# One-hots of the first index moved to ScalarE in every batch, the build and the dense stage re-placed in the row order

## The chip, the core and the metric

The kernel runs on one core of a Trainium2 chip. The core has TensorE (PE), VectorE (DVE), ScalarE (ACT), GpSimd (POOL) and SyncE (SP), which run side by side and meet at semaphores, and 16 DMA engines that all queues share. The metric is the device time of one execution in microseconds (us); lower is better.

## What is computed

A one-layer streaming encoder in float32 for 512 prompt tokens and 64 sample tokens, width 2048: retention and mLSTM heads, then the PEER expert mixer, then gated per-layer embeddings. The change touches the expert mixer. For every token, 8 heads pick 16 of 16384 experts each (128 picks); the expert number is `i1 * 128 + i2`. Cut to what matters:

```
eidx = i1 * N_KEYS + i2            # (T, 128) expert numbers, N_KEYS = 128
act  = gelu(einsum('td,tkd->tk', xb, u[idx]))      # one row of peer_u for each pick
out  = einsum('tk,tkd->td', g * act, v[idx])       # one row of peer_v for each pick
```

## The kernel before

Tokens lie in 5 blocks of 128 (block 4 is the sample block, its 64 tokens laid out twice, so it has 64 picks per partition). A "row" is one pick of all 128 tokens of a block: GpSimd gathers 128 vectors of 2048 floats from `peer_u` (1 MiB) into a slot of `ring`. VectorE takes the dot product with the token (L2330), and for blocks 0, 3 and 4 it later adds the gathered row of `peer_v` to the token's sum (L2342, 12 rows behind). Rows are numbered 0 to 575; block 2 is rows 256 to 383, block 3 rows 384 to 511, block 4 rows 512 to 575. From row 384 on the `peer_u` rows use three slots of the ring and the `peer_v` rows three others.

Blocks 1 and 2 (`DENSE`) do without the second gather. Their weights are made dense: for each token a matrix of 128 x 128 (first index by second index) that holds the weight of each picked expert. This is the **build**. It goes in batches of four tokens, 32 batches (`PER`) for each of the two blocks, `b` 0 to 63. A batch is:

- VectorE compares the indices with `iota` and makes one-hots (L2204). In even batches it makes those of both indices (128 x 1024), in odd ones only those of the second (128 x 512).
- ScalarE makes the first index's one-hots in odd batches as `relu(1 - |index - iota|)`: four Abs (L1644) and one Relu (L1647). It then scales the second one-hots by the weights, four instructions (L1657).
- TensorE multiplies the two (L1206), ScalarE copies the product of the batch before out of psum (L1679).
- Every four batches 1 MiB goes to `a_scratch` in HBM, half issued by SP and half by ACT (L764).

Three sets of one-hot buffers go round (`SETS`), so the compare of batch `b` waits for the multiplication of batch `b - 2` (L2201), and so do ScalarE's Abs.

The **dense stage** then reads all of `peer_v` once, in 32 groups `m` of four 1 MiB tiles. For each group TensorE multiplies tiles by weights (L1223) in four parts, VectorE adds each part (L2221), and SP loads the group after next only when a group is done. Weights come back in 16 chunks (L783). TensorE is at most three parts ahead of VectorE. After the dense stage comes the gated embedding product of blocks 0 to 3 (`pe_embed`, L1265) in four groups, whose sigmoids are ScalarE's (L1725) and whose sums are VectorE's (L2240, L2244).

Each engine runs one stream of instructions in order, written by weaving several generators (`braid`). A step yields a place in row numbers, and the step with the lowest place is written next. `BUILD_AT` gives for each dense block the first row and the rows per batch, `DENSE_AT` the first row of the dense stage and the rows per group, `EMBED_AT`, `EMBED_RS` and `GROUP_ROWS` the places of the embedding's steps. So these numbers set only the order on VectorE and ScalarE; how long it takes is decided by waits.

Of the kernel before, what the change touches and what calls it, by code (L numbers as in the profile page):

```python
# [14 lines left out]
P = 128  # L15
# [45 lines left out]
BATCH = 4  # L61
# [8 lines left out]
ALONE = (128, 384)  # L70

CHAIN_AT = {0: (-89, 4.0), 1: (12, 4.7), 2: (138, 8.7)}
EMBED_AT = {0: (533, 1.05), 1: (700, 1.0)}
FIRST_PICK = {1: 4.0, 2: 10.0}
LATE_PICKS = {1: [(131, 10), (148, 16), (170, 18), (200, 18), (222, 18), (246, 18), (270, 18)],
              2: [(402, 9), (424, 18), (450, 20), (472, 9), (481, 9), (490, 9), (499, 9)]}
BUILD_AT = ((352, 0.9), (390, 0.55))
DENSE_AT = (412, 3.75)
GROUP_ROWS = (548.5, 10.5)
EMBED_RS = 541.5  # L80

def in_at(g, x):
# [44 lines left out]
def build_at(d, x):  # L128
    return BUILD_AT[d][0] + BUILD_AT[d][1] * x

def dense_at(x):
    return DENSE_AT[0] + DENSE_AT[1] * x

def embed_at(e, x):
    return EMBED_AT[e][0] + EMBED_AT[e][1] * x

# [221 lines left out]
def build(nc, a, out):  # L360
    with ExitStack() as ctx:
# [41 lines left out]
        def bank(n, width=512):  # L403
            return psum[:, n, 0:width]

        far, ident, keep, fold = (misc[:, x:x + P] for x in (M_FAR, M_ID, M_KEEP, M_FOLD))
        iota, iota_p, one = misc[:, M_IOTA:M_IOTA + NC], misc[:, M_IOTA:M_IOTA + P], misc[:, M_ONE:M_ONE + 1]
# [148 lines left out]
        def one_hots(b):  # L556

            at = 1024 + b % SETS * 1024
            return (X if b >= PER else Wf)[:, at:at + 1024].rearrange("p (f t i) -> p f t i", f=2, t=BATCH)
# [9 lines left out]
        def stored(i, w):  # L569

            return 32 * len(range(i, w, SETS))
# [80 lines left out]
        f0 = y0 = len(EMBEDS[0])  # L652
# [984 lines left out]
        def act_build(act):  # L1637
            def first_hots(d, b):

                if b >= SETS:  # L1640
                    act.wait_ge(a_mm, b - SETS + 1)
                for x in range(BATCH):
                    t = b % PER * BATCH + x
                    ins = act.activation(one_hots(b)[:, 0, x, :], iota_p, ACT.Abs, bias=build_parts(d)["indexT"][:, t:t + 1], scale=-1.0)  # L1644
                act_o.did(ins)
                act_o.wait()
                act_o.did(act.activation(one_hots(b)[:, 0], one_hots(b)[:, 0], ACT.Relu, bias=1.0, scale=-1.0))  # L1647

            def weigh(d, b):

                if b % 2:
                    first_hots(d, b)
                act.wait_ge(hots, b + 1)
                for x in range(BATCH):
                    t = b % PER * BATCH + x
                    hot = one_hots(b)[:, 1, x, :]
                    ins = act.activation(hot, hot, ACT.Identity, scale=build_parts(d)["weightT"][:, t:t + 1])  # L1657
                ins.then_inc(weighed, 1)
            for d in range(len(DENSE)):
                yield build_at(d, -1)  # L1660
                act.wait_ge(index_t, d + 1)
                act.copy(build_parts(d)["indexT"], bank(6)[:, 0:2 * P])
                act.copy(build_parts(d)["weightT"], bank(7)[:, 0:P]).then_inc(index_c, 1)
                for i in range(PER + 1):
                    b = d * PER + i
                    if i < PER:
                        yield build_at(d, i + 0.1)
                        if i == 0:
                            act.wait_ge(index_c, d + 1)
                        weigh(d, b)  # L1670
                    if i == 0:
                        continue
                    b -= 1
                    yield build_at(d, i + 0.2)
                    act.wait_ge(a_mm, b + 1)
                    w, t0 = b // WRITE, b % WRITE * BATCH
                    if w >= SETS and t0 == 0:
                        act.wait_ge(a_out[w % SETS], stored(w % SETS, w))
                    act.copy(a_stage(w)[:, :, t0:t0 + BATCH, :].rearrange("p c t k -> p t c k"),  # L1679
                             bank(b % 4).rearrange("p (t c k) -> p t c k", t=BATCH, k=CHUNK)).then_inc(a_c, 1)  # L1680
                    if b % WRITE == WRITE - 1:
                        act.wait_ge(a_c, b + 1)
                        store_a(act, w, 1)
# [14 lines left out]
        def act_embed(act):  # L1698
# [4 lines left out]
            for q in range(4):  # L1703
                for j, t in enumerate(ts):
# [7 lines left out]
                    act.activation(spare, hrow(t), ACT.Square, accum_out=ncol(i, 0)).then_inc(n_sq, 1)  # L1712
            yield EMBED_RS
            act.wait_ge(n_ms, rooted(counts.stat["ple", 0, 0]))
# [463 lines left out]
        def dve_build(dve):  # L2178
            o = dve_o
            for d, t in enumerate(DENSE):  # L2180
                parts = build_parts(d)
                yield build_at(d, -2)
                if d:
                    dve.wait_ge(moved, 2)
                    dve.wait_ge(picked[3], 1)
                else:
                    dve.wait_ge(mm, prod.end("q", 2))
                dve.wait_ge(weighted, (ROW0[t] + ROWS[t]) // GRP)
                o.wait()
                o.did(dve.tensor_scalar(parts["first_u"].bitcast(U32), eidx[:, eslot(t), :], 7, None, ALU.logical_shift_right))  # L2190
                o.did(dve.tensor_scalar(parts["second_u"].bitcast(U32), eidx[:, eslot(t), :], NKEY - 1, None, ALU.bitwise_and))
                o.wait()
                o.did(dve.tensor_copy(parts["first_f"], parts["first_u"].bitcast(U32)))
                dve.tensor_copy(parts["second_f"], parts["second_u"].bitcast(U32)).then_inc(split, 1)
                for i in range(PER):
                    b = d * PER + i
                    yield build_at(d, i)
                    if i == 0:
                        dve.wait_ge(index_c, d + 1)
                    if b >= SETS:  # L2200
                        dve.wait_ge(a_mm, b - SETS + 1)  # L2201
                    index = parts["indexT"].rearrange("p (f t o) -> p f t o", f=2, o=1)[:, :, i * BATCH:(i + 1) * BATCH, :]
                    f0 = b % 2
                    dve.tensor_tensor(one_hots(b)[:, f0:, :, :], index[:, f0:, :, :].to_broadcast([P, 2 - f0, BATCH, P]),  # L2204
                                      iota_p.rearrange("p (a b i) -> p a b i", a=1, b=1).to_broadcast([P, 2 - f0, BATCH, P]),
                                      ALU.is_equal).then_inc(hots, 1)

        def dve_dense(dve):
# [14 lines left out]
        def dve_embed(dve):  # L2223
            ts, n = EMBEDS[0], len(EMBEDS[0])

            def at(x):
                return embed_at(0, x)
            yield EMBED_RS
            dve.wait_ge(n_sq, counts.stat["ple", 0, n - 1] + 1)
            dve.tensor_scalar(embed_cols(1), embed_cols(0), 1.0 / D, EPS, ALU.mult, ALU.add).then_inc(n_ms, 1)  # L2230
            yield EMBED_RS + 0.6
            dve.wait_ge(n_rt, rooted(counts.stat["ple", 0, 0]))
# [147 lines left out]
```

## Time and profile before

| | us |
|---|---|
| median of 3 runs | 3673.85 (3673.23 to 3678.76) |
| the profiled execution, its own time | 3674.24 |
| span of its instructions | 3672.4 |
| PE busy | 3098.5 |
| VectorE busy | 2748.2 |
| GpSimd busy | 1301.3 |
| ScalarE busy | 642.8 |

The span is the time from the first to the last instruction; 1.8 us lie around it. Busy times overlap, since the engines run side by side. All times below are counted from the start of the span. The DMA engines moved 1453.00 MB in all.

### The profile page before, as it was taken

To read this page: it belongs to the slowest core of one execution; us is meant where nothing else is said; L and a number is where in the kernel's file an instruction comes from. 1 tells how busy PE (TensorE), PEld (TensorE's weight loads), DVE (VectorE), ACT (ScalarE), POOL (GpSimd) and SP (SyncE) were. 2 spreads that over 40 slices of the span, in tenths; PEclk is the share of its full clock that TensorE was granted. 3 is DMA by queue.
4 is the path that set the end of the run, shared out by engine and by line. 5 is a ranking of instruction groups with operands and counts; after the bars stand their busy time and mean duration, and the time that the engine had idled before them with its cause. 6 is when DMAs were issued, how large, how long until landed. Compare 5 with 4: busy or idle time off the path is not lost.

```text
span 3672.4 us, 26507 instructions
## 1 busy us (share of the span) xinstructions
PE 3098.5 (84%) x9234; PEld 1897.2 (52%) x9234; DVE 2748.2 (75%) x3646; ACT 642.8 (18%) x1694; POOL 1301.3 (35%) x908
## 2 busy tenths in 40 slices
PE   8998697999988189899897545699999999799697
PEld 4447443554456144455347544466666666574343
DVE  1014987767668799888778888878788999777885
ACT  2211210222011031122202367200000000003002
POOL 0001542424335443323234533432323323342771
PEclk9999799999989589999898755699999999899899
DMA  8889999999999999999999999999999999999998
GB/s 272 282 274 326 418 417 417 419 417 419 418 413 407 381 390 417 417 418 384 378 416 404 400 383 388 389 421 422 421 421 422 419 421 418 389 421 415 417 401 354
DMA packets 310517, 1453.00 MB, mean 396 GB/s; under 512 B 26032, under 2 KB 64368, under 8 KB 172272
## 3 DMA queue, kind: packets, MB, share of 16 engines
q0 software_dynamic: 129840, 944.83, 62.9%
q1 hardware_dynamic: 153728, 485.39, 34.4%
q10 hardware_dynamic: 26816, 21.09, 1.7%
q8 instruction: 73, 1.20, 0.1%
q14 instruction: 60, 0.49, 0.0%
HBM read 1424.48 MB, written 26.74 MB: 395 GB/s over the span
## 4 chain that ended last, share of the span: by engine, by line
DMA 44%; DVE 18%; PE 14%; issue 6%; POOL 4%; ACT 1%; DVEq 0%; SPq 0%; ACTq 0%
DMA ring<-in_peer_u,eidx 23%; DMA ring<-in_peer_v,eidx 15%; DVE ring L2330 8%; DMA W<-in_w_peer_q 5%; PE psum L911 5%; DVE arena L2342 4%; POOL ring L843 4%; PE psum L1265 3%; PE psum L1223 3%; PE psum L1174 1%; DVE arena L2221 1%; DMA a_scratch<-W 1%; PE psum L1312 1%; DMA W<-in_w_out 1%; DVE arena L2204 1%
## 5 line engine op out<-in xcount | busy, mean ns | idle before, releaser
L2330 DVE CUSTOM_DVE_ANT_0 ring<-ring,cx 128x2048 f32<-128x2048 f32 x576 | 1315.2, 2287 | 301.5 <-DMA ring<-in_peer_u,eidx 298.6
L843 POOL DMA_INDIRECT ring<-in_peer_u,eidx x576 | 825.3, 1433 | 1609.9 <-DVE dots L2330 1194.1
L2342 DVE SCALAR_TENSOR_TENSOR arena<-ring,wts,arena 128x2048 f32<-128x2048 f32 x320 | 752.3, 2351 | 185.0 <-DMA ring<-in_peer_v,eidx 156.8
L911 PE MATMUL psum<-W,actT 128*128 128x512 f32 x1792 | 799.7, 605 | 45.3 <-ACT actT L858 21.0
L843 POOL DMA_INDIRECT ring<-in_peer_v,eidx x320 | 470.8, 1471 | 671.9 <-DVE arena L2342 633.4
L911 PEld LDWEIGHTS psum<-W,actT 128*128 128x128 f32 x1792 | 344.6, 194 | 467.6 <-issue 449.9
L1174 PE MATMUL psum<-actT,W 128*128 128x128 f32 (+2 forms) x1536 | 293.4, 356 | 97.8 <-DMA W<-in_w_peer_q 89.0
L1174 PEld LDWEIGHTS psum<-actT,W 128*128 128x128 f32 x1536 | 267.4, 211 | 123.3 <-DMA W<-in_w_peer_q 97.1
L1796 ACT ACTIVATE gel<-dots 128x8 f32<-128x8 f32 x72 | 15.2, 212 | 1610.1 <-DVE dots L2330 1605.6
L1223 PE MATMUL psum<-arena 128*128 128x512 f32 x512 | 233.0, 614 | 36.2 <-DVE arena L2221 36.2
L911 PE MATMUL psum<-W,arena 128*128 128x512 f32 x512 | 230.9, 612 | 21.1 <-DMA W<-in_w_out 20.6
L1223 PE MATMUL psum<-W,actT 128*128 128x512 f32 x512 | 225.8, 601 | 21.2 <-DMA actT<-a_scratch 16.9
L1223 PE MATMUL psum<-arena,actT 128*128 128x512 f32 x512 | 226.2, 600 | 12.0 <-DVE arena L2221 12.0
L1223 PE MATMUL psum<-W,arena 128*128 128x512 f32 x512 | 225.0, 599 | 8.6 <-DVE arena L2221 8.6
L1223 PEld LDWEIGHTS psum<-arena 128*128 128x128 f32 x512 | 159.9, 315 | 108.3 <-DVE arena L2221 41.4
L1223 PEld LDWEIGHTS psum<-W,actT 128*128 128x128 f32 x512 | 159.9, 314 | 85.9 <-issue 25.6
L1223 PEld LDWEIGHTS psum<-arena,actT 128*128 128x128 f32 x512 | 159.8, 314 | 76.8 <-DVE arena L2221 17.3
L889 PE MATMUL psum<-W,actT 128*128 128x512 f32 x448 | 198.8, 602 | 0.0
L1223 PEld LDWEIGHTS psum<-W,arena 128*128 128x128 f32 x512 | 159.9, 314 | 72.7 <-issue 10.5
L911 PEld LDWEIGHTS psum<-W,arena 128*128 128x128 f32 x512 | 99.7, 197 | 148.3 <-issue 120.8
L2221 DVE TENSOR_TENSOR arena<-psum,arena 128x1024 f32<-128x1024 f32 x128 | 155.9, 1218 | 18.0 <-PE psum L1223 17.9
L1265 PE MATMUL psum<-W,actT 128*128 128x512 f32 x256 | 118.3, 614 | 32.5 <-ACT arena L1725 32.5
(332 smaller groups left out, 2526.8 us busy)
## 6 DMA issues: line engine op xcount, KB each, us to landing
W<-in_w_in SPq DMA_DIRECT2D x168, 1024.0 KB, 12.3
W<-in_peer_v SPq DMA_DIRECT2D x64, 1024.0 KB
arena<-in_peer_v SPq DMA_DIRECT2D x64, 1024.0 KB, 16.8
W<-in_w_out SPq DMA_DIRECT2D x48, 1024.0 KB, 16.7
W<-in_w_peer_q SPq DMA_DIRECT2D x48, 1024.0 KB, 27.7
W<-in_w_ple_gate SPq DMA_DIRECT2D x24, 1024.0 KB, 16.0
ring<-in_peer_u,eidx POOLq DMA_INDIRECT x576, 18.2
actT<-a_scratch SPq DMA_DIRECT2D x8, 1024.0 KB, 28.0
```

What stands on the lines that cost most here:

```text
L843: pool.indirect_dma_start(ring[:, slot, :], None, a["peer_u" if what == "u" else "peer_v"][0], off(ix, 0)).then_inc(ring_in[slot], 16)
L889: ins = pe.matmul(bank(4 * s + j), lhs(k, j), W[:, k, :], start=(k == 0), stop=(k == KT - 1))
L911: ins = pe.matmul(bank(4 * s + j), lhs(at_k, j), w_pair(q)[:, k, s * CG:(s + 1) * CG], start=(at_k == 0), stop=(at_k == KT - 1))
L1174: ins = pe.matmul(bank(2 * (i % 2) + c // 2)[:, at:at + fresh], W[:, k, c * P:(c + 1) * P], actT[:, k, 0:fresh], start=(k == 0 and c % 2 = ...
L1223: ins = pe.matmul(bank(at % 3 * 2 + half), a_chunk(c)[:, i // 2 * P:(i // 2 + 1) * P, m * VT % CHUNK + x], v_tiles(m)[:, x, c0:c0 + 512], ...
L1265: ins = pe.matmul(bank(j), aT(k, j), W[:, k, :], start=(k == 0), stop=(k == KT - 1))
L1312: ins = pe.matmul(psum[SAMPLE * b:SAMPLE * (b + 1), s, :], actT[:, k, 0:SAMPLE], w_row(k)[:, cols_of(s, b)], start=(k == 0), stop=(k == KT ...
L1796: act.activation(gel[:, n % DEEP, :], dots[:, n % DEEP, :], ACT.Gelu).then_inc(gelud, 1)
L2204: dve.tensor_tensor(one_hots(b)[:, f0:, :, :], index[:, f0:, :, :].to_broadcast([P, 2 - f0, BATCH, P]), iota_p.rearrange("p (a b i) -> p a ...
L2221: dve.tensor_tensor(hc, psum[:, at % 3 * 2:at % 3 * 2 + 2, :], hc, ALU.add).then_inc(d_add, 1)
L2330: dve.tensor_tensor_reduce(row, row, cx[:, :], 1.0, 0.0, ALU.mult, ALU.add, dots[:, n % DEEP, c:c + 1]).then_inc(u_used, 1)
L2342: dve.scalar_tensor_tensor(out=hslot(t), in0=ring[:, slot, :], scalar=wts[:, n % DEEP, c:c + 1], in1=hslot(t), op0=ALU.mult, op1=ALU.add). ...
```

## The change

Four numbers of the order change, and the one-hots of the first index are ScalarE's in all batches.

```
-EMBED_AT = {0: (533, 1.05), 1: (700, 1.0)}
+EMBED_AT = {0: (536, 1.05), 1: (700, 1.0)}
...
-BUILD_AT = ((352, 0.9), (390, 0.55))
-DENSE_AT = (412, 3.75)
+BUILD_AT = ((352, 1.15), (396, 0.7))
+DENSE_AT = (423, 3.5)
...
-EMBED_RS = 541.5
+EMBED_RS = 543.5
...
             def weigh(d, b):
 
-                if b % 2:
-                    first_hots(d, b)
+                first_hots(d, b)
                 act.wait_ge(hots, b + 1)
...
-                    f0 = b % 2
-                    dve.tensor_tensor(one_hots(b)[:, f0:, :, :], index[:, f0:, :, :].to_broadcast([P, 2 - f0, BATCH, P]),
-                                      iota_p.rearrange("p (a b i) -> p a b i", a=1, b=1).to_broadcast([P, 2 - f0, BATCH, P]),
+                    dve.tensor_tensor(one_hots(b)[:, 1:, :, :], index[:, 1:, :, :].to_broadcast([P, 1, BATCH, P]),
+                                      iota_p.rearrange("p (a b i) -> p a b i", a=1, b=1).to_broadcast([P, 1, BATCH, P]),
                                       ALU.is_equal).then_inc(hots, 1)
```

In the changed file lines after the ScalarE edit are one lower, those after the VectorE edit two lower.

VectorE's stream at the first batches of block 1 (row 352). `W` holds the one-hots; an ISA row with `ring,dots` is one `peer_u` row. Before:

```order
L2204 TENSOR_TENSOR W<-W,misc 128x1024
L2204 TENSOR_TENSOR W<-W,misc 128x512
L2330 ISA ring,dots<-ring,cx 128x2048
L2330 ISA dots 128x1
L2204 TENSOR_TENSOR W<-W,misc 128x1024
```

In the changed kernel:

```order
L2202 TENSOR_TENSOR W<-W,misc 128x512
L2328 ISA ring,dots<-ring,cx 128x2048
L2328 ISA dots 128x1
L2202 TENSOR_TENSOR W<-W,misc 128x512
L2328 ISA ring,dots<-ring,cx 128x2048
```

Every compare is now of the short form, and with 1.15 rows per batch two seldom stand together; the last four batches of block 1 move behind the start of block 3 at row 384.

VectorE's stream at the first batches of block 2 (`arena` holds the one-hots there). Before:

```order
L2204 TENSOR_TENSOR arena<-arena,misc 128x1024
L2204 TENSOR_TENSOR arena<-arena,misc 128x512
L2330 ISA ring,dots<-ring,cx 128x2048
L2330 ISA dots 128x1
L2204 TENSOR_TENSOR arena<-arena,misc 128x1024
L2204 TENSOR_TENSOR arena<-arena,misc 128x512
```

In the changed kernel:

```order
L2202 TENSOR_TENSOR arena<-arena,misc 128x512
L2334 TENSOR_TENSOR wts<-gel,gate 128x8
L2340 SCALAR_TENSOR_TENSOR arena<-ring,wts,arena 128x2048
L2202 TENSOR_TENSOR arena<-arena,misc 128x512
L2328 ISA ring,dots<-ring,cx 128x2048
L2328 ISA dots 128x1
L2202 TENSOR_TENSOR arena<-arena,misc 128x512
```

Two compares stood between two `peer_u` rows (rows 390 to 396 have no `peer_v` rows yet); now the compares begin at row 396, among rows of both kinds.

ScalarE's stream at the first batches of block 1. Before:

```order
L1657 ACTIVATE W<-W 128x128 x4
L1644 ACTIVATE W<-misc,W 128x128 x4
L1647 ACTIVATE W<-W 128x512
L1657 ACTIVATE W<-W 128x128 x4
L1679 COPY W<-psum 128x4x16x8
L1657 ACTIVATE W<-W 128x128 x4
L1679 COPY W<-psum 128x4x16x8
```

In the changed kernel:

```order
L1644 ACTIVATE W<-misc,W 128x128 x4
L1647 ACTIVATE W<-W 128x512
L1656 ACTIVATE W<-W 128x128 x4
L1644 ACTIVATE W<-misc,W 128x128 x4
L1647 ACTIVATE W<-W 128x512
L1656 ACTIVATE W<-W 128x128 x4
L1678 COPY W<-psum 128x4x16x8
```

Abs and Relu now stand ahead of every scaling. The dense stage's first sum moves from row 412.94 to 423.88, its last from row 532 to 535, and the embedding's ScalarE steps and its root follow by 3 and 2 rows.

## Rows read from the trace of the kernel before

**Rows 1.** The page: busy time of the engines and their shares.

```profile
PE 3098.5 (84%) x9234; PEld 1897.2 (52%) x9234; DVE 2748.2 (75%) x3646; ACT 642.8 (18%) x1694; POOL 1301.3 (35%) x908
```

**Rows 2.** Stretches: length, busy PE, PEld, DVE, ACT, POOL; PE clock, DMA share, GB/s.

```profile
2084.00:2187.00 103.00, 60.83 (x256) 53.72 (x256) 99.84 (x101) 84.18 (x243) 42.24 (x30) 0.58 1.02 392
2187.00:2244.00 57.00, 17.54 (x75) 15.67 (x75) 38.63 (x42) 23.42 (x70) 21.04 (x16) 0.53 0.95 355
2244.00:2352.00 108.00, 51.05 (x193) 41.99 (x193) 106.66 (x148) 65.11 (x181) 48.38 (x32) 0.53 1.02 388
2352.00:2441.00 89.00, 89.00 (x208) 64.87 (x207) 62.76 (x46) 0.21 (x1) 29.95 (x23) 1.00 1.01 421
...
3160.00:3200.00 40.00, 20.60 (x44) 13.22 (x43) 30.21 (x22) 0.00 (x0) 18.10 (x12) 0.74 0.92 361
3200.00:3315.00 115.00, 114.73 (x275) 83.36 (x273) 89.97 (x66) 1.80 (x4) 45.22 (x31) 1.00 1.01 419
```

**Rows 3.** VectorE's compares, by form, 2084 to 2336 us (busy, mean ns, idle before).

```profile
L2204 DVE TENSOR_TENSOR W<-W,misc 128x1024 f32<-128x1024 f32 x16 | 19.7, 1231 | 0.8 <-PE psum L1206 0.8
L2204 DVE TENSOR_TENSOR arena<-arena,misc 128x1024 f32<-128x1024 f32 x16 | 19.5, 1221 | 2.9 <-PE psum L1206 2.9
L2204 DVE TENSOR_TENSOR W<-W,misc 128x512 f32<-128x512 f32 x16 | 11.1, 693 | 2.2 <-PE psum L1206 2.2
L2204 DVE TENSOR_TENSOR arena<-arena,misc 128x512 f32<-128x512 f32 x16 | 11.0, 687 | 1.9 <-PE psum L1206 1.9
```

**Rows 4.** VectorE in order of time (start, us; in brackets idle before and releaser).

```profile
2184.78 2.35 DVE L2306 SCALAR_TENSOR_TENSOR cx<-arena,stat,ring 128x2048 f32<-128x2048 f32 x1
...
2215.44 2.29 DVE L2330 CUSTOM_DVE_ANT_0 ring<-ring,cx 128x2048 f32<-128x2048 f32 x1 [2.66 <-DMA ring<-in_peer_u,eidx]
...
2236.97 1.23 DVE L2204 TENSOR_TENSOR arena<-arena,misc 128x1024 f32<-128x1024 f32 x1 [1.21 <-PE psum L1206]
```

**Rows 5.** ScalarE in order of time, one odd batch, then the restart after a store.

```profile
2087.00 1.27 ACT L1644 ACTIVATE W<-misc,W 128x128 f32<-128x128 f32 x4
2088.30 0.63 ACT L1647 ACTIVATE W<-W 128x512 f32<-128x512 f32 x1
2088.84 1.26 ACT L1657 ACTIVATE W<-W 128x128 f32<-128x128 f32 x4
2090.01 0.56 ACT L1679 COPY W<-psum 128x512 f32<-128x512 f32 x1
2090.47 1.28 ACT L1657 ACTIVATE W<-W 128x128 f32<-128x128 f32 x4
...
2098.01 0.59 ACT L1679 COPY W<-psum 128x512 f32<-128x512 f32 x1 [0.51 <-PE psum L1206]
...
2099.14 1.28 ACT L1644 ACTIVATE W<-misc,W 128x128 f32<-128x128 f32 x4 [0.54 <-ACT W L1679]
```

**Rows 6.** DMA queues, 2114 to 2146 us (packets, MB, share of 16 engines): gathers, then stores.

```profile
q0 software_dynamic: 1439, 10.50, 77.9%
q1 hardware_dynamic: 2605, 1.31, 13.6%
q10 hardware_dynamic: 2465, 1.24, 12.9%
```

**Rows 7.** TensorE in order of time: block boundary, one dense group, embedding's start and groups.

```profile
3180.34 23.18 PE L1223 MATMUL psum<-arena 128*128 128x512 f32 x48 [19.40 <-DVE arena L2221]
3203.36 27.63 PE L1223 MATMUL psum<-W,actT 128*128 128x512 f32 x64
...
3316.05 1.53 PE L850 MATMUL psum<-misc,arena 128*128 128x128 f32 x12 [1.32 <-DVE arena L2221]
...
3391.10 9.85 PE L1265 MATMUL psum<-W,actT 128*128 128x512 f32 x16 [4.10 <-ACT arena L1725]
...
3484.30 9.34 PE L1265 MATMUL psum<-W,actT 128*128 128x512 f32 x16 [28.41 <-ACT arena L1725]
```

**Rows 8.** VectorE in order of time: first embedding sum.

```profile
3420.13 0.68 DVE L2240 TENSOR_TENSOR arena<-psum,arena 128x512 f32<-128x512 f32 x1
```

## The prediction

> **What bounds the kernel now.** I read the page first. Over the whole span TensorE is busy 84%, VectorE 75%, ScalarE 18% [rows 1]. No engine is full, so I looked at stretches. In the dense stage, 2352 to 2441 us, the DMA engines have a share of 1.01 and move 421 GB/s while VectorE is busy 62.8 of 89 us [rows 2]. I take 421 GB/s as what the DMA engines give when they are full, and the row stream there as bound by them. In the three stretches of the build they move 392, 355 and 388 GB/s [rows 2]. VectorE is busy 99.8 of 103 us in the first and 106.7 of 108 us in the third. In the second, rows 384 to 396 (the start is the new `cx` after row 383 [rows 4]), it is busy 38.6 of 57 us and waits now for DMA (2.66 us), now for TensorE's product before a compare (1.21 us) [rows 4]. So the build is where time is lost, to a full VectorE and to waits, and all else is bytes.
>
> How much is lost: the three stretches move 103 x 0.392 + 57 x 0.355 + 108 x 0.388 = 102.5 MB in 268 us. At 421 GB/s that is 243.5 us, so 24.5 us are missing. Part of it is the price of the stores to `a_scratch`, which come in packets of 1.31 MB / 2605 = 503 bytes [rows 6]. In 32 us two store queues moved 2.55 MB and took 13.6 + 12.9 = 26.5% of the engines, 8.5 us: 300 GB/s. But gathers took 77.9%, and the shares add up to more than 100%; what the gathers leave is 7.1 us, 359 GB/s. The 16 MiB of stores (16.8 MB) thus cost 47 to 56 us against 40 at full rate, 7 to 16 us more, and that part stays. **True idle time of DMA is 8.4 to 17.6 us**, and it is the most that the change can give.
>
> **The change part by part.**
>
> *VectorE.* 32 long compares of 1231 and 1221 ns become short ones of 693 and 687 ns [rows 3]: 32 x 0.54 = 17.2 us less work. The waits in front of the compares for TensorE are 0.8 + 2.9 + 2.2 + 1.9 = 7.8 us in all.
>
> *ScalarE.* 32 more sets of Abs and Relu. An odd batch (Abs, Relu, scaling, copy) takes 2090.47 - 2087.00 = 3.47 us [rows 5]. After a store the copy's start lies 2099.14 - 2098.01 = 1.13 us before the next instruction, against 0.46 us otherwise, so 0.17 us per batch more. Every batch now costs 3.64 us, 116 us per block. This ends up on the path only if rows come faster than ScalarE makes batches, since the compare of batch b waits for the product of b - 2.
>
> *Rows 352 to 384 (103 us now).* 28 instead of 32 batches stand here. VectorE's compares fall from 19.7 + 11.1 = 30.8 us to 28 x 0.69 = 19.4, and its 3.0 us of waits may go: 89 us of need. DMA moves 40.4 MB less half a store pair of 1.1 MB, 39.3; 7.3 of it stores at 300 to 359 GB/s (24 to 20 us) and 32.0 at 421 (76 us): 96 to 100 us. ScalarE must have finished batch 25 before the last compare ahead of row 384: 26 x 3.64 = 95 us, and 2 to 5 us for its start and for late stores: 97 to 100 us. VectorE stops being the bound and two others stand just behind it. I take 99: **4 us less**, with bounds of 0 (ScalarE a little slower) and 7.
>
> *Rows 384 to 396 (57 us now).* The compares of block 2 leave this stretch, with their waits for TensorE; four late batches of block 1 come in at one per 1.15 rows, not two per 1.1. About the same 20.2 MB go through (12 `peer_u` rows, a load of `cx`, four tiles, the last stores), which at full rate takes 48 us. But here the `peer_u` rows have three slots alone, and when nothing else is loading three cannot fill the DMA engines. I take 52: **5 us less**, bounds 0 and 8.
>
> *Rows 396 to 423 (108 + 89 = 197 us now).* Now the dense stage begins at row 412 and by row 423 some two more groups of tiles have been loaded than with the change; those bytes are only moved later. The change leaves 27 x 2.10 = 56.6 MB of rows, 8.4 of stores, four tiles and two chunks 6.3: 71.3 MB, 173 to 177 us. VectorE loses another 8.5 us of compares and has room. Now 41.9 + 37.5 = 79.4 MB go in 197 us, 71.8 of them (with some 7.6 of stores) no stores: 171 + 21 to 25 = 192 to 196. The idle time here is 1 to 5 us; I take **3 us less**, bounds 0 and 5.
>
> *Dense stage.* One group moves 4.19 MB of tiles, half a chunk 0.52, and 3.5 rows of 2.10 MB each: 12.05 MB, 28.6 us at 421 GB/s. Now, with 3.75 rows, it is 12.58 MB and 29.9 us. TensorE needs 27.63 us for a group [rows 7], so its slack falls from 2.3 to 1.0 us per group. At the block boundary (row 512) VectorE waits for a new `cx` and TensorE stood for 19.4 us [rows 7], the DMA rate was 361 GB/s over 40 us [rows 2]; afterwards TensorE worked 114.7 of 115 us. It will now catch up more slowly. I put **1 to 2 us more** on it, bounds 0 and 25 (below).
>
> *Embedding.* The last dense sum moves by three rows, 6.3 MB or 15 us, less the 12 us won before: about 3 us later than the 3315 us of now (TensorE turns at 3316.05 [rows 7]). The first embedding group's sigmoids were out before TensorE went on at 3391.10 [rows 7], and VectorE first used them at 3420.13 [rows 8]: 29 us of cover. The third group waited 28.41 us for ScalarE, whose stream holds it until row 559 [rows 7]. Shifts up to 28 us cost nothing; that wait shrinks. The moved ScalarE and root steps stay ahead of their users and I cost them at 0; without the cover each us late is a us at the end. From row 559 on everything hangs on the rows.
>
> **Sum.** 4 + 5 + 3 - 2 = 10 us less. Against the profiled execution's 3674.24 us (0.4 us over the median of the runs) that is **3664 us**.
>
> **The rivals.**
>
> *DMA was full anyway (no change to be measured).* VectorE's cut buys nothing where the share is already 1.02 [rows 2]. With the stores at 300 GB/s only 8 us are idle, and if three slots keep rows 384 to 396 as they are, 3 us remain: 3671, in a span of 3667 to 3677. For it: the shares. Against: 355 GB/s at a share of 0.95 in the second stretch, and VectorE almost without a gap in the two others. Chance 0.27. The Trainium skill (Perfetto Trace Analysis, Identifying the Most-Contended Engine) says that the engine with the highest occupancy, or DMA, is the one to work on, and by that rule, since DMA leads over the span, this change is worth nothing; the same section allows that the contended engine changes over time, as the stretches show.
>
> *TensorE becomes the dense stage's bound (slower).* The dense stage now lasts 963 us, 32 x 27.63 = 884 of them work and 79 waiting for VectorE's sums. The start moves to about 2390 us. If the 79 us stay, the last sum is at 3353, 35 us later than the 3318 above. In its queue the rows stand behind the sums, so they come late too and DMA runs empty: up to 25 us, 3689. It decides from a mean period of (3318 - 2390) / 32 = 29.0 us per group. For it: the 1 us of slack, TensorE without a gap after the boundary. Against: those waits are for sums placed late in VectorE's order, and with 0.875 instead of 0.94 rows between sums they shrink by themselves. Chance 0.12.
>
> *ScalarE becomes the build's bound (slower or same).* If a batch takes 4.3 us instead of 3.64 (a wait in front of the copies for late stores, a product at TensorE's low clock of 0.58 [rows 2]), 26 batches take 112 us and rows 352 to 384 last 9 us more than now, while VectorE waits at L2201 with the rows behind it. With 3 us from the last stretch and 5 us lost at row 384, 3674 + 9 + 5 - 3 = 3685. It decides from 3.9 us per batch, where the first stretch stays at 103. For it: 97 to 100 us of need against 96 to 100 of DMA. Against: the odd batches show no such wait. Chance 0.11.
>
> **The numbers.** The forecast, a gain of 6 to 19 us (3655 to 3668), has a chance of 0.50. I call 0.2%, 7.3 us, what a measurement of this kernel tells from no change. Almost all of the forecast's chance and a sliver of the first rival's lie below 3666.5: faster 0.52, same 0.29, slower 0.19. The range 3655 to 3685 leaves out one in ten on the side of the bounds (17.6 us of idle all recovered) and one on the side of a bound TensorE.
>
> **What would show it.** Right: the last `peer_u` row before 384 ends near 2183 us; VectorE has gaps of DMA in rows 352 to 384, where it had none; waits before compares near zero; rows 384 to 396 take near 52 us; the dense period is 28.6 us and TensorE turns near 3318; the wait at the third embedding group is near 25 us. Wrong: VectorE waiting before the short compares for L1206 over 5 us in a block (ScalarE is the bound), VectorE waiting before the dense sums for more than some 40 us (TensorE is), or GB/s in the three stretches as now (DMA was full).

## The result and the profile after

The changed kernel takes 3688.36 us (median of 6 runs, 3683.87 to 3695.08); the kernel before takes 3674.14 us beside it (6 runs). The ratio is 1.004 (95% interval 1.0026 to 1.0053): 14 us slower, where 10 us faster were forecast. A second set of runs of the changed kernel gave 3685.35 (10 runs, beside 3674.91; ratio 1.0026, 1.0014 to 1.0037). The profiled execution of the changed kernel has a span of 3686.2 us.

The page of the changed kernel, engine line, and then its stretches, which stand beside [rows 1] and [rows 2]:

```profile
PE 3091.1 (84%) x9234; PEld 1907.2 (52%) x9234; DVE 2731.8 (74%) x3646; ACT 696.9 (19%) x1853; POOL 1296.9 (35%) x908
```

```profile
2084.00:2187.00 103.00, 53.20 (x205) 45.46 (x206) 96.61 (x108) 94.53 (x272) 66.17 (x32) 0.51 0.98 383
2187.00:2244.00 57.00, 17.42 (x68) 14.65 (x68) 38.89 (x40) 28.84 (x84) 24.34 (x18) 0.50 0.98 366
2244.00:2352.00 108.00, 47.87 (x186) 41.10 (x186) 104.50 (x152) 83.21 (x235) 54.29 (x32) 0.50 1.00 389
2352.00:2441.00 89.00, 31.68 (x95) 23.86 (x95) 58.02 (x52) 26.71 (x74) 52.60 (x24) 0.56 0.98 395
2435.00:2455.00 20.00, 20.00 (x48) 14.56 (x48) 19.79 (x28) 0.00 (x0) 5.70 (x5) 1.00 0.66 225
3160.00:3200.00 40.00, 28.52 (x64) 19.58 (x63) 32.39 (x24) 0.00 (x0) 11.58 (x12) 0.87 1.01 420
```

VectorE has 16.4 us less work (17.2 were costed) and ScalarE 54 more. But the build moves its bytes no faster: 383, 366 and 389 GB/s where it was 392, 355 and 388. And the stretch 2435 to 2455, where the kernel before moves 422 GB/s, now moves 225. VectorE's compares, and the sums of the dense stage (2400 to 3345 us), in the changed kernel, beside [rows 3]:

```profile
L2202 DVE TENSOR_TENSOR W<-W,misc 128x512 f32<-128x512 f32 x32 | 22.0, 689 | 6.1 <-PE psum L1206 5.9
L2202 DVE TENSOR_TENSOR arena<-arena,misc 128x512 f32<-128x512 f32 x32 | 21.9, 683 | 0.0
...
L2219 DVE TENSOR_TENSOR arena<-psum,arena 128x1024 f32<-128x1024 f32 x128 | 155.9, 1218 | 58.0 <-PE psum L1223 57.9
```

Of the 58 us that VectorE waits before sums, 26 are one wait. SyncE's issues, TensorE, VectorE and GpSimd around it, in order of time, in the changed kernel:

```profile
2381.98 0.36 SPq L764 DMA_DIRECT2D a_scratch<-arena  x1
2416.47 0.33 SPq L783 DMA_DIRECT2D actT<-a_scratch  x1
```

```profile
2379.26 2.08 PE L1206 MATMUL psum<-arena 128*128 128x128 f32 x8 [1.40 <-ACT arena L1656]
2425.52 29.96 PE L1223 MATMUL psum<-W,actT 128*128 128x512 f32 x64 [44.19 <-DMA actT<-a_scratch]
```

```profile
2406.63 2.35 DVE L2340 SCALAR_TENSOR_TENSOR arena<-ring,wts,arena 128x2048 f32<-128x2048 f32 x1 [0.59 <-DMA ring<-in_peer_v,eidx]
2434.99 1.23 DVE L2219 TENSOR_TENSOR arena<-psum,arena 128x1024 f32<-128x1024 f32 x1 [26.01 <-PE psum L1223]
```

```profile
2410.09 0.94 POOL L843 DMA_INDIRECT ring<-in_peer_v,eidx  x1 [0.30 <-issue]
2438.69 0.94 POOL L843 DMA_INDIRECT ring<-in_peer_u,eidx  x1 [27.66 <-DVE dots L2328]
```

Read it as a chain. The last pair of stores to `a_scratch` is issued at 2381.98. SP waits for all stores before it reads the first weight chunk back, and goes on only at 2416.47, 34.5 us later. The chunk lands, and TensorE makes its first dense product at 2425.52. VectorE has been at its first dense sum since 2408.98 and waits 26 us. All rows stand behind that sum in its queue, no slot of the ring comes free, GpSimd issues nothing for 27.66 us, and what was queued for DMA runs out. In the kernel before, SP's wait was 6.4 us, and the sum did not wait:

```profile
2329.80 0.36 SPq L764 DMA_DIRECT2D a_scratch<-arena  x1
2336.18 0.33 SPq L783 DMA_DIRECT2D actT<-a_scratch  x1
2358.68 1.22 DVE L2221 TENSOR_TENSOR arena<-psum,arena 128x1024 f32<-128x1024 f32 x1
```

From the last issue of a store to VectorE's arrival at the first sum it is 28.9 us before (2329.80 to 2358.68) and 27.0 us now (2381.98 to 2408.98). That distance is nearly the same. What has changed is the landing of the stores in between.

**A ledger of lost time.** To compare versions I take, at the start of a `peer_u` row on VectorE, the time so far less the bytes that the DMA engines have moved so far, divided by 421.5 GB/s. What it grows by in a stretch is time in which DMA was not moving bytes at its full rate; the higher price of the small store packets is part of it. The program moves 1453 MB in all, so the span is this sum plus 3447 us. Worked out from the packets of each profile, in us, by stretches between rows. Some versions have a second profile, of another execution:

| version | to 352 | 352 to 423 (build) | 423 to 427 (first sums) | 427 to 508 | 508 to 540 | 540 to end | span |
|---|---|---|---|---|---|---|---|
| before | 169.4 | 25.4 | -0.1 | 1.4 | 8.4 | 20.6 | 3672.4 |
| before again | 173.6 | 24.8 | 0.0 | 1.7 | 8.1 | 20.4 | 3675.9 |
| before again, second profile | 168.2 | 25.7 | 0.0 | 1.6 | 8.1 | 21.0 | 3671.8 |
| changed | 176.3 | 22.7 | **11.4** | 0.6 | 5.3 | 22.5 | 3686.2 |
| changed again | 172.5 | 25.9 | **10.8** | 0.5 | 5.8 | 20.8 | 3683.7 |
| one-hots only | 170.2 | **47.0** | 0.0 | 1.6 | 8.3 | 20.6 | 3695.1 |
| one-hots only, second profile | 163.4 | **46.5** | 0.0 | 1.8 | 8.6 | 21.0 | 3688.8 |
| places only | 166.9 | 23.3 | **9.5** | 0.5 | 5.5 | 21.6 | 3674.7 |
| places only, second profile | 172.2 | 31.1 | **9.7** | 0.5 | 5.1 | 24.2 | 3690.1 |
| dense from 428 | 171.0 | 24.1 | -0.1 | 0.7 | **16.7** | 17.6 | 3677.3 |
| dense from 428, second profile | 170.1 | 23.7 | 0.0 | 0.8 | **18.2** | 18.0 | 3678.2 |
| dense place only | 173.2 | 22.2 | 0.0 | 0.7 | 5.2 | 22.7 | 3671.3 |
| vector load | 173.5 | **40.4** | -0.1 | 0.9 | 4.3 | 23.6 | 3690.0 |
| build early | 171.1 | 20.9 | 0.0 | 1.1 | 5.2 | 21.0 | 3666.6 |
| build early again | 170.4 | 20.2 | -0.1 | 0.8 | 5.6 | 23.2 | 3667.4 |
| places early | 171.5 | 21.0 | 0.0 | 1.3 | 4.9 | 22.3 | 3668.3 |
| six slots | 167.7 | **53.3** | -0.1 | 1.2 | 5.3 | 23.2 | 3698.0 |
| early, one queue | 175.0 | 22.4 | 0.3 | 0.4 | 5.6 | 21.1 | 3672.2 |

All versions are the same program up to row 352, so the first column, 163.4 to 176.3, is chance from one execution to the next. One profile against one profile can be off by that much. Between profiles of one version the three middle columns repeat to 1.5 us and the last to some 2.5. The column of the build repeats to some 3 us, but for "places only" it is 23.3 in one and 31.1 in the other.

By the means of two profiles each (the first two lines of before), the span grows by 10.8 us: 11.1 at the first sums and 1.2 at the end, less 2.7 at the block boundary, 1.0 ahead of it and 0.8 in the build; the 2.9 us left lie ahead of anything changed. So the changed parts account for 7.8 us. The medians say 14 us, and 10 in the second set of runs; where the other 3 to 6 us lie, these profiles do not show.

### The profile page after: what moved, and what is told of

Read it like the earlier page. It is cut to its first block, busy times and chain, and to the rows that moved or that the text cites. A ratio compares the mean times of both kernels' runs of the same rounds, so it can differ in the third digit from the quotient of the medians.

```text
span 3686.2 us, 26665 instructions
## 1 busy us (share of the span) xinstructions
PE 3091.1 (84%) x9234; PEld 1907.2 (52%) x9234; DVE 2731.8 (74%) x3646; ACT 696.9 (19%) x1853; POOL 1296.9 (35%) x908
## 4 chain that ended last, share of the span: by engine, by line
DMA 46%; PE 17%; DVE 13%; issue 5%; ACT 3%; POOL 3%; ACTq 0%; SPq 0%; DVEq 0%
DMA ring<-in_peer_u,eidx 23%; DMA ring<-in_peer_v,eidx 14%; PE psum L911 6%; DMA W<-in_w_peer_q 6%; DVE ring L2328 5%; PE psum L1223 4%; POOL ring L843 3%; DVE arena L2340 3%; PE psum L1265 3%; DMA W<-in_w_out 2%; PE psum L1174 1%; DMA a_scratch<-arena 1%; ACT W L1656 1%; PE psum L1312 1%; ACT W L1644 1%
## 5 line engine op out<-in xcount | busy, mean ns | idle before, releaser
L911 PE MATMUL psum<-W,actT 128*128 128x512 f32 x1792 | 801.3, 606 | 49.0 <-ACT actT L858 23.1
L911 PEld LDWEIGHTS psum<-W,actT 128*128 128x128 f32 x1792 | 344.9, 195 | 472.5 <-issue 453.6
L1223 PE MATMUL psum<-W,actT 128*128 128x512 f32 x512 | 227.7, 605 | 53.1 <-DMA actT<-a_scratch 44.2
L911 PE MATMUL psum<-W,arena 128*128 128x512 f32 x512 | 227.1, 604 | 23.8 <-DMA W<-in_w_out 22.2
L1223 PE MATMUL psum<-arena 128*128 128x512 f32 x512 | 222.8, 594 | 4.0 <-DVE arena L2219 4.0
L1223 PEld LDWEIGHTS psum<-W,actT 128*128 128x128 f32 x512 | 159.9, 314 | 119.9 <-issue 55.8
L2219 DVE TENSOR_TENSOR arena<-psum,arena 128x1024 f32<-128x1024 f32 x128 | 155.9, 1218 | 58.0 <-PE psum L1223 57.9
L889 PE MATMUL psum<-W,actT 128*128 128x512 f32 x448 | 197.4, 599 | 0.0
L889 PEld LDWEIGHTS psum<-W,actT 128*128 128x128 f32 x448 | 85.4, 193 | 102.2 <-issue 101.9
```

The lines of the kernel that those rows point to most:

```text
L889: ins = pe.matmul(bank(4 * s + j), lhs(k, j), W[:, k, :], start=(k == 0), stop=(k == KT - 1))
L911: ins = pe.matmul(bank(4 * s + j), lhs(at_k, j), w_pair(q)[:, k, s * CG:(s + 1) * CG], start=(at_k == 0), stop=(at_k == KT - 1))
L1223: ins = pe.matmul(bank(at % 3 * 2 + half), a_chunk(c)[:, i // 2 * P:(i // 2 + 1) * P, m * VT % CHUNK + x], v_tiles(m)[:, x, c0:c0 + 512], ...
L2219: dve.tensor_tensor(hc, psum[:, at % 3 * 2:at % 3 * 2 + 2, :], hc, ALU.add).then_inc(d_add, 1)
```

## The experiments

**The kernel before once more** (no edit). How far do two executions differ ahead of the build?

> The kernel before, unchanged, for a second profile. If the 7 us by which the changed kernel's profile is behind at row 352, ahead of every changed instruction, are chance between executions, this profile differs from the first one at row 352 by several us too. If they belong to the change, it repeats the first within 1 us (2082 us).

3677.71 us; row 352 began at 2087.0 us, 4.7 later than in the first profile, and in a second profile of this run at 2081.5. The lateness of the changed kernel at row 352 is of that size.

**Dense stage later.** In the changed kernel:

```
-DENSE_AT = (423, 3.5)
+DENSE_AT = (428, 3.34)
```

> The changed kernel with DENSE_AT (428, 3.34) in place of (423, 3.5): the first dense sum stands at row 428.8, the last still at 535. Theory A (the loss is the wait of 26 us at the first sum, because the last stores to a_scratch land 34 us after their issue and SP loads the first chunk only then): the wait falls from 26 us to under 5 and 9 to 11 us come back, 3677. Theory B (the thin slack of TensorE in the dense stage is the loss): the denser sums make it worse or leave it, 3688 or more.

3681.73 us (10 runs, ratio to before 1.0023, 1.0012 to 1.0034). That is 4 to 7 us less than the changed kernel, where 9 to 11 were expected. Nothing is lost at the first sums any more, but 16.7 us at the block boundary where the others lose 4 to 9, and L2219 still waits 55.5 us for TensorE. With a group every 3.34 rows TensorE needs all its time (27.63 us, against 27.8 of transfers for 4.71 MB and 3.34 rows of 2.10 MB) and cannot catch up behind row 512. Both theories had a part of it: 5 rows remove the stall, and a tighter rate brings the TensorE bound of the second rival.

**The two parts apart.** First the kernel before with ScalarE's one-hots alone, its places as before:

```
-                if b % 2:
-                    first_hots(d, b)
+                first_hots(d, b)
...
-                    f0 = b % 2
-                    dve.tensor_tensor(one_hots(b)[:, f0:, :, :], ...
+                    dve.tensor_tensor(one_hots(b)[:, 1:, :, :], ...
```

> The kernel before with only ScalarE's one-hots in all batches; all places in the row order as before. ScalarE needs 3.6 us a batch and the places give 3.1: both theories expect VectorE to wait for TensorE ahead of the compares and, by theory A, a wait of 20 to 40 us at the first dense sum at row 412.9; 3685 to 3700. If the wait at the first sum is under 10 us and the time is that of before, theory A is wrong about where the stores are late.

3697.99 us (4 runs, ratio 1.0062, 1.0038 to 1.0086), slower than the full change, and for another reason than I expected. Nothing waits at the first sum in the profile shown here (7.2 us in a second one, at no loss); SP went on 12 us after the last issue. The time goes in the build, 47.0 instead of 25 us. VectorE's compares there:

```profile
L2202 DVE TENSOR_TENSOR W<-W,misc 128x512 f32<-128x512 f32 x32 | 22.0, 691 | 24.5 <-PE psum L1206 24.5
L2202 DVE TENSOR_TENSOR arena<-arena,misc 128x512 f32<-128x512 f32 x32 | 21.9, 688 | 17.0 <-PE psum L1206 16.9
```

41.4 us of waits where [rows 3] have 7.8: at 0.9 and 0.55 rows per batch ScalarE is too slow (it is busy 98.60 of the 103 us from 2084), and the rows stand behind the compare. This is the third rival, in a version with the old places.

Then the four places alone, VectorE still making the first one-hots of even batches (the four number lines of the change's diff, no other edit):

> The kernel before with only the places changed (BUILD_AT, DENSE_AT, EMBED_AT, EMBED_RS as in the changed kernel); VectorE still makes the first index's one-hots in even batches. Theory A: VectorE is nearly full from row 396 to 418 and holds back the gathers, so the last stores land in about 10 us and there is no long wait at the first sum; 3670 to 3676. Theory B (the places with 3.5 rows per group are at fault): 3686 or more, as the changed kernel.

3684.08 us (10 runs, ratio 1.0023, 1.0012 to 1.0035). My expectation fell: the stall is there all the same. SP issues the last stores at 2374.6 and goes on at 2405.96, TensorE waits 41.3 us, the sums 65.0 us, and 9.5 us are lost at rows 423 to 427. (That execution was the fastest of the ten.) In a second profile the last stores are issued at 2387.84, SP goes on at 2419.27, and 9.7 us are lost. VectorE is busy in all 14 us ahead of those stores (2374 to 2388), and still DMA moves 410 GB/s and GpSimd gathers almost without a pause. So the places make the stall, not ScalarE's work, and a full VectorE alone does not hold the gathers back.

**The changed kernel once more** (no edit).

> The changed kernel, unchanged, for more times and a second profile. All theories: 3684 to 3692; the first dense sum again waits 20 to 30 us and the same 9 to 12 us of DMA time are lost there.

3685.35 us. The stall repeats: TensorE waits 44.42 us for the chunk, VectorE 65.8 us before sums, 10.8 us lost.

**Build of block 2 five rows earlier.** In the changed kernel:

```
-BUILD_AT = ((352, 1.15), (396, 0.7))
+BUILD_AT = ((352, 1.15), (391, 0.7))
```

> The changed kernel with the compares of block 2 from row 391 (BUILD_AT ((352, 1.15), (391, 0.7))): five rows more between the last store and the first dense sum at row 423.9, the dense rate of 3.5 untouched. Theory A (stores that land late hold the first chunk): the wait at the first sum falls under 8 us and 8 to 11 us come back, 3676 to 3680. Theory B (the dense rate): still 3685 or more.

3669.43 us (10 runs, ratio 0.9991, 0.9981 to 1.0001), 16 us under the changed kernel, and 3671.07 in a second set (12 runs, ratio 0.999, 0.9976 to 1.0003; expectation below). That is 7 us better than expected: the 11 us of the first sums come back and the build loses some 4 less. The stores land no sooner (last issue 2352.6, SP on at 2387.75, 35 us; 33 us in the second profile), but now VectorE arrives after them: TensorE begins at 2398.08, and VectorE is at its first sum at 2414.26, without a wait.

> e_build_early again, for a narrow interval against the kernel before: 3667 to 3671, ratio 0.998 to 0.999.

**Dense stage's and embedding's places alone**, on the kernel before:

```
-EMBED_AT = {0: (533, 1.05), 1: (700, 1.0)}
+EMBED_AT = {0: (536, 1.05), 1: (700, 1.0)}
...
-DENSE_AT = (412, 3.75)
+DENSE_AT = (423, 3.5)
...
-EMBED_RS = 541.5
+EMBED_RS = 543.5
```

> The kernel before with only the dense stage's places changed (DENSE_AT (423, 3.5), EMBED_AT 536, EMBED_RS 543.5); the build is as before and ends at row 407. Theory A: no wait at the first sum, the time of before or up to 3 us more (3672 to 3678). Theory B: the sums at 3.5 rows per group cost by themselves, above all behind row 512 where TensorE catches up; 3682 or more.

3675.33 us (10 runs, ratio 1.0001, 0.9989 to 1.0012): no change. A group per 3.5 rows costs nothing; the block boundary even loses 5.2 instead of 8.4 us. The rate is thus not what costs. Nor did the change bring the build nearer to the dense stage in the row order: from the last batch's place to the first sum it is 5.9 rows before, 6.2 in the changed kernel, 11.2 in "build early", 11.1 in "dense from 428" and 16.8 here. Six rows were enough while the stores landed in 6 us.

**VectorE loaded with useless compares** in the second half of block 2's build, results untouched. In the changed kernel, ahead of its compare (L2202):

```
+                    if d and i >= PER // 2:
+                        o.did(dve.tensor_tensor(psum[:, 4:6, :]..., index.to_broadcast([P, 2, BATCH, P]), iota_p..., ALU.is_equal))
+                        o.wait()
```

> The changed kernel with a useless compare of 1.2 us into two free psum banks ahead of each of the last 16 compares of block 2 (rows 407 to 418), so that VectorE and no longer DMA paces the rows there; results are untouched. If stores land late because gathers keep the DMA engines full, the last ones land within 12 us of their issue here, not 34, and the wait at the first sum falls to 5 us or less although the rows come some 10 us later: 3682 to 3690. If the stores land late for a reason of their own, they still take about 30 us and the wait stays near 20 us.

3691.81 us (one run). The last stores were issued at 2400.7 and SP went on at 2406.55, 5.9 us later; the sums wait 8.5 us. The version takes longer, since VectorE holds the rows back, but it bears on the wait: stores land soon when few gathers are queued, and late when gathers are queued without end.

The packets show how. DMA queues in the time from about the last issue to SP's going on (packets, MB, share of the engines; q0 are the gathers, q1 and q10 the stores of SP and ScalarE). The kernel before, 2329.8 to 2336.2 us:

```profile
q0 software_dynamic: 143, 1.04, 51.9%
q1 hardware_dynamic: 1040, 0.52, 27.1%
q10 hardware_dynamic: 1040, 0.52, 27.1%
```

The changed kernel, 2382 to 2416 us, and then 2387 to 2412 us of it alone:

```profile
q0 software_dynamic: 1720, 12.54, 87.4%
q10 hardware_dynamic: 1616, 0.81, 7.9%
q1 hardware_dynamic: 1585, 0.80, 7.8%
```

```profile
q0 software_dynamic: 1255, 9.11, 86.3%
q10 hardware_dynamic: 1256, 0.63, 8.4%
q1 hardware_dynamic: 1255, 0.63, 8.4%
```

A pair of stores is 2 x 1040 packets of 504 bytes. In the changed kernel some 550 packets of the pair before were still there in each queue. For 25 us each of the three queues gets the same number of packets, 50 per us, though a gather packet has 7.3 KB. At 50 per us the 1600 of a store queue take 32 us, and it took 34.5. Where the gathers are held back, the same pair needs 6 us. The Trainium skill (DMA: Bandwidth & Descriptors, Queues, rings and completion order) has each DMA engine take turns between the queues that have work, a packet at a time, where its packet is a bundle of descriptors. The equal counts agree with turns; how its bundles relate to the packets of the profile no run here shows.

The totals alone mislead. The version "places early" (below) took 21 us, in which 1027 gather packets pass and 1040 in each store queue, but not one for one. Its first 5 us, 2355 to 2360:

```profile
q0 software_dynamic: 167, 1.23, 58.4%
q1 hardware_dynamic: 899, 0.46, 30.5%
q10 hardware_dynamic: 501, 0.26, 17.1%
```

There few gathers were queued at first, and what comes later are the last packets of a pair: 141 and 539 in 15.6 us. "Build early" has such a tail too. In the first 19.4 us 990 and 969 packets of the two store queues pass beside 974 gather packets, and the last 187 and 254 take 15.7 us. So a landing has two parts, the turns and a tail in which the gathers get most of the engines' time.

GpSimd shows the same from its side. Its gathers in the kernel before, and in the changed kernel, at the time of the last stores:

```profile
2324.05 1.14 POOL L843 DMA_INDIRECT ring<-in_peer_u,eidx  x1 [1.86 <-DVE dots L2330]
2326.92 1.44 POOL L843 DMA_INDIRECT ring<-in_peer_v,eidx  x1 [1.72 <-DVE arena L2342]
2332.07 2.80 POOL L843 DMA_INDIRECT ring<-in_peer_u,eidx  x1 [3.71 <-DVE dots L2330]
```

```profile
2384.17 2.62 POOL L843 DMA_INDIRECT ring<-in_peer_u,eidx  x1 [0.30 <-issue]
2387.10 2.52 POOL L843 DMA_INDIRECT ring<-in_peer_v,eidx  x1 [0.30 <-issue]
2389.92 2.69 POOL L843 DMA_INDIRECT ring<-in_peer_u,eidx  x1 [0.30 <-issue]
```

Before, each gather waits for VectorE to free a slot; with the change slots are free and GpSimd gathers without a pause.

**The early places, one-hots as before.** All four places of "build early", on the kernel before, VectorE making both one-hots of even batches:

```
...
-BUILD_AT = ((352, 0.9), (390, 0.55))
-DENSE_AT = (412, 3.75)
+BUILD_AT = ((352, 1.15), (391, 0.7))
+DENSE_AT = (423, 3.5)
...
```

> The kernel with all places of e_build_early (BUILD_AT ((352, 1.15), (391, 0.7)), DENSE_AT (423, 3.5)), but VectorE still makes the first index's one-hots in even batches: what the move to ScalarE is worth when nothing stalls. Theory A (DMA is full in the build, so 17 us less VectorE work buys little): the same as e_build_early within 4 us, 3668 to 3674. If VectorE's work is what bounds the build, as the prediction had it: 8 to 14 us slower than e_build_early, 3677 to 3683.

3670.07 us (10 runs, ratio 0.9984, 0.9974 to 0.9994), the same as "build early" (3669.43, and 3671.07 beside this version). Its stretches:

```profile
2084.00:2187.00 103.00, 54.85 (x229) 48.19 (x230) 102.97 (x103) 75.71 (x219) 73.78 (x32) 0.58 1.02 395
2187.00:2244.00 57.00, 24.36 (x104) 20.85 (x102) 41.91 (x45) 33.43 (x98) 28.09 (x18) 0.56 1.00 386
```

VectorE is full in the first, 102.97 of 103 us, and yet 395 GB/s flow, no less than with ScalarE's help. The move of the one-hots, on its own, is worth nothing here.

**Six slots for all rows up to 396**, on "build early": can more slots fill DMA in rows 384 to 396?

```
-ALONE = (128, 384)
+ALONE = (128, 396)
```

> e_build_early with ALONE (128, 396): the peer_u rows 384 to 395, which have no peer_v rows beside them, go through six slots of the ring and not three. Theory: three slots in flight cannot fill the DMA engines there; of the 8 to 9 us of DMA time lost in rows 384 to 396 some 4 to 6 come back, 3664 to 3667. Rival (the loss there is the change of block, cx, and the stores' price): within 2 us of e_build_early.

3699.28 us (4 runs, ratio 1.0058, 1.004 to 1.0076), 30 us over "build early": a clear miss. Rows 384 to 396 lose 6.1 us instead of 7.7, but rows 396 to 412 lose 41. A stretch and GpSimd's gathers in it:

```profile
2230.00:2310.00 80.00, 26.99 (x104) 23.16 (x104) 48.00 (x61) 45.00 (x128) 20.74 (x19) 0.50 0.74 263
```

```profile
2276.44 1.14 POOL L843 DMA_INDIRECT ring<-in_peer_u,eidx  x1 [11.88 <-DVE arena L2340]
2277.88 0.94 POOL L843 DMA_INDIRECT ring<-in_peer_v,eidx  x1 [0.30 <-issue]
2289.11 0.94 POOL L843 DMA_INDIRECT ring<-in_peer_u,eidx  x1 [10.29 <-DVE arena L2340]
```

A `peer_u` gather needs a slot that a `peer_v` row holds, VectorE uses that row late in its order, and GpSimd, which issues in order, stands. Three slots for each kind, switched at row 384 when the `peer_v` rows restart, keep the two from blocking each other. Which slot assignment would serve rows 384 to 396 better was not tried.

**Both halves of the last store from one queue**, on "build early": bytes and packets as before, but 2080 packets in SP's queue and none in ScalarE's.

```
                 store_a(sp, w, 0)
+                if w == writes - 1:
+                    store_a(sp, w, 1)
...
-                    if b % WRITE == WRITE - 1:
+                    if b % WRITE == WRITE - 1 and b < NBATCH - 1:
```

> The kernel with the build of block 2 from row 391 on (its time was 3669.43), and of the last write of the weights SP now issues both halves (two times 1040 packets of about 500 bytes), ScalarE none. The bytes and the packets stay as they were. Theory: while gathers are queued without end, each store queue gets about one packet for every 1.0 to 1.6 gather packets of 7.3 KB, whatever the size of its packets, so a store's landing is set by the number of its packets in one queue. There the last pair was issued at 2352.6 us and SP went on at 2387.75, 35 us later; 1040 more packets in one queue are 20 us or more, so SP goes on 55 us or more after the last issue, near 2407; TensorE begins near 2416 and VectorE, which reaches its first dense sum near 2414, waits 10 to 20 us for it; some us are added to the time (3672 to 3682). Rival: the stores land late because they stand behind all gathers issued before them, or take their share by bytes, and the number of queues is nothing to them: SP goes on 33 to 38 us after the last issue, VectorE does not wait, and the time is 3664 to 3674.

3673.96 us (one run; before took 3677.89 beside it). SP's issues:

```profile
2358.63 3.49 SPq L764 DMA_DIRECT2D a_scratch<-arena  x2
2403.59 0.33 SPq L785 DMA_DIRECT2D actT<-a_scratch  x1
```

The last issue began at 2359.0, so SP went on 44.6 us later, not 33 to 35 and not 55. The number of packets in one queue matters, but by half of what was expected. While both queues are full they again get the same counts (2369 to 2384 us):

```profile
q0 software_dynamic: 810, 5.90, 93.0%
q1 hardware_dynamic: 810, 0.41, 9.1%
```

That is 54 per us where three queues got 50 each, and "build early" had spent 15 of its 35 us in the tail. VectorE waits 12.65 us for TensorE at the first sum, as expected, which costs only 0.3 us, since DMA did not run dry.

## Why the prediction was wrong

**The start of the dense stage: the step that failed.** The prediction moved it "to about 2390 us" and gave it no cost. It took the weights to be back when VectorE arrives, so the landing of the last stores stood at nothing in the sum. The row that bears on it, TensorE's first dense product, waited 16.89 us in the kernel before, and I had not traced what stands behind it: last copy, last store, its landing, SP's wait, the chunk. From the last store's issue to SP's read of the chunk it was 6.4 us and is 34.5 now; from that read to the first product it was 9.9 us and is 9.1. TensorE started at 2425.5. VectorE's own distance from store to sum stayed at 27 to 29 us, so a landing 28 us later became a wait of 26, and that costs 11.1 us. "Places only" shows that the new places bring the late landing, without ScalarE's work. The build at 0.7 and not 0.55 rows per batch has fewer compares per row, which lets more gathers queue; that this is the reason is argued, and no run tests it by itself.

**The build, "12 us less": 0.8 measured.** Per stretch, lost time before and changed (means of two profiles): rows 352 to 384, 7.8 and 6.9 (forecast 4 less); rows 384 to 396, 8.6 and 8.6 (5 less); rows 396 to 423, 8.7 and 8.8 (3 less). A single stretch repeats only to 3 us, so these are no change. The compares did become short, but VectorE's cut bought nothing, as the first rival ("DMA was full anyway") has it. "Places early", with VectorE full, loses just 4.2 us in the first stretch; but "dense place only", which has there the instructions of the kernel before, loses 4.7 where that one lost 7.9, so this can be chance. The idle time of 8.4 to 17.6 us was too large a prize: the best builds lose 20 to 21 us and the kernel before 25, so that some 4 us of it were had, and by the places. How much of that is chance stays open.

Two readings behind this term were off, at no harm to the result. L2201 lets the compare of batch b go when b - 2 products are done, so it waits for batch b - 3, not b - 2, and ScalarE needed 25 batches, 91 us, and not 95. And rows 384 to 396 moved 16 MB in the changed kernel, not the 20.2 put down, since the first four tiles are loaded later.

**The dense stage's slack, "1 to 2 us more": 2.7 less.** The boundary loses 5.5 instead of 8.2 us, in the changed kernel and in all versions at 3.5 rows per group. The fear of a tight TensorE was right only at 3.34 rows (16.7 and 18.2).

**Embedding, 0.** TensorE turned at 3344.75, 29 us later than before, and the third group's wait fell from 28.41 to 20.65 us: the cover held. The end lost 1.2 us more, within what repeats.

**The rivals.** The time, 3688, is that of "TensorE becomes the dense stage's bound" (3689), and its sign came true: VectorE waited 58 us before sums, over the 40 given. Its mechanism did not, and that the time agrees is luck: TensorE's period is (3344.75 - 2425.52) / 32 = 28.7 us, under the 29.0 from which it was to decide. TensorE started 35 us late and then waited just 25 us for VectorE, where it waited 61 before. Of VectorE's 58 us, 26 are the stall. The other 32 cost nothing that the ledger shows (0.6 and 0.5 us lost in rows 427 to 508, where 1.4 and 1.7 were).

The sign of the third rival came true too, by a little: VectorE waited 5.9 us for L1206 in block 1, over the 5 given, and 0 in block 2. ScalarE was near its limit in block 1, busy 94.53 of 103 us, but the build lost no more than before. With the old places it is the bound ("one-hots only").

The Trainium skill (Perfetto Trace Analysis, Identifying the Most-Contended Engine) says to optimize the most contended engine first. The first rival took from it that relief of VectorE is worth nothing while DMA leads, and "places early" against "build early" agrees: 3670.07 and 3671.07 us, side by side.

**In short:** a gain of 2.7 at the boundary and nothing clear in the build, a loss of 11 at the first dense sum. "Places early", with ratio 0.9984, is the best version run, though not told apart from "build early"; it needs the new places with the build five rows earlier, and none of the change on ScalarE.

## What to carry to other kernels

When a producer and its consumer are moved together, the distance between them can stay and still become too short. Follow the whole chain between them, the landing of the last store included, and compare its end with the moment when the first engine in order gets there. A landing measured while few other transfers are queued is no measure for a landing in a full queue: here 6 us became 35. And an order in which rows stand behind a wait turns every us of it, once the slots are used up, into idle DMA.

## What the hardware showed that I had not expected

- A store of 2 x 0.52 MB in packets of 504 bytes lands after 6 us where 143 gather packets pass, after 21 us where 1027 do, and after 31 to 36 us where 1600 or more do. Its price in DMA time is about the same, 3.5 us of all 16 engines (54.2% of 6.4 us before, 17.0% of 20.6 us in "places early"); only its landing moves.
- With all queues full, gathers in packets of 7.3 KB and stores in packets of 504 bytes pass in equal numbers: 1255, 1256 and 1255 in 25 us.
- With both halves of the last store in one queue it landed 9 to 12 us later at the same bytes (one run). The last 8 us before the landing in "build early" carried only 81 store packets among 446 gather packets; whether single DMA engines lag behind the others there is not recorded in the trace and stays open.
- Executions of the same instructions differ by up to 13 us of lost time by row 352, more than most effects studied here.
